# Sums of squares of queries and keys as two products of a rounded high part and a rest

## The reference, cut to what matters

```
h = rmsnorm(x, norm1_g[i])
u = h @ w_in[i]
...
heads = lambda t: t.reshape(b, s, ATTN_HEADS, HEAD_DIM)
qf = rmsnorm(heads(q), q_g).astype(jnp.float32) * (HEAD_DIM ** -0.5)
kf = rmsnorm(heads(k), k_g).astype(jnp.float32)
```

## Time and profile before

| | us |
|---|---|
| median of 3 runs | 1605.55 (1605.2 to 1606.04) |
| the profiled execution, its own time | 1606.08 |
| span of its trace | 1604.2 |
| PE busy in the span | 1580.6 (99%) |
| DVE, ACT, POOL busy | 909.7, 762.8, 645.4 |

### The profile page before, as it was taken

The page is one execution under the profiler, slowest core; times in us unless marked ns, Lnnn a source line. Parts: engine busy times, 40 slices in busy tenths (PEclk is TensorE's granted clock), DMA queues, the critical chain, the costliest instruction groups (busy, mean ns, idle before and its releaser), DMA issues.

```text
span 1604.2 us, 19275 instructions
## 1 busy us (share of the span) xinstructions
PE 1580.6 (99%) x7352; PEld 1262.7 (79%) x7352; DVE 909.7 (57%) x1310; ACT 762.8 (48%) x1204; POOL 645.4 (40%) x323
## 2 busy tenths in 40 slices
PE   7999999999999999999999999999999999999999
PEld 5776778787878888888877777787878788888887
DVE  4578859577755555522227788586678554554000
ACT  5557667476343333332244666765744433333221
POOL 3432221223445555554443312213144555555443
PEclk9999999999999999999999999999999999999999
DMA  5532144453223233233324222454532233232333
GB/s 169 132 100 93 49 124 145 145 150 100 92 92 103 93 98 99 92 95 99 95 92 132 89 76 66 121 157 135 153 98 92 93 94 103 93 102 92 98 96 112
DMA packets 57371, 170.86 MB, mean 107 GB/s; under 512 B 5984, under 2 KB 11872, under 8 KB 57280
## 3 DMA queue, kind: packets, MB, share of 16 engines
q1 hardware_dynamic: 56896, 168.88, 34.0%
q0 software_dynamic: 384, 0.75, 0.4%
HBM read 166.24 MB, written 3.38 MB: 106 GB/s over the span
## 4 chain that ended last, share of the span: by engine, by line
PE 84%; DMA 5%; DVE 3%; issue 3%; POOL 2%; ACT 1%; SPq 1%; DVEq 0%; POOLq 0%; ACTq 0%
PE banks L1170 25%; PE banks L1172 25%; PE banks L1171 25%; DMA sb_w_raw<-w_in 3%; PE banks L1257 2%; PE banks L1248 2%; PE banks L1268 2%; DMA sb_e<-sum_rows 1%; PE banks L1320 1%; PE banks L1228 1%; POOL sb_xc L474 1%; DVE sb_w_lo L847 1%; SPq L339 1%; ACT sb_w_hi L527 0%; DMA sb_x_stream<-x_t 0%
## 5 line engine op out<-in xcount | busy, mean ns | idle before, releaser
L439 POOL TENSOR_TENSOR sb_w_lo<-sb_w_raw,sb_w_hi 128x1024 fp32r<-128x1024 f32 x200 | 482.1, 2411 | 598.9 <-ACT sb_w_hi L527 598.9
L527 ACT ACTIVATE sb_w_hi<-sb_w_raw 128x1024 fp32r<-128x1024 f32 x256 | 271.2, 1059 | 700.1 <-PE banks L1172 648.7
L1170 PE MATMUL banks<-sb_h_hi,sb_w_hi 128*128 128x512 f32 x1344 | 541.7, 403 | 13.1 <-POOL sb_w_lo L439 11.4
L1171 PE MATMUL banks<-sb_h_lo,sb_w_hi 128*128 128x512 f32 x1344 | 524.4, 390 | 0.0
L1172 PE MATMUL banks<-sb_h_hi,sb_w_lo 128*128 128x512 f32 x1344 | 524.4, 390 | 0.0
L1170 PEld LDWEIGHTS banks<-sb_h_hi,sb_w_hi 128*128 128x128 f32 x1344 | 252.7, 188 | 85.2 <-issue 29.7
L1171 PEld LDWEIGHTS banks<-sb_h_lo,sb_w_hi 128*128 128x128 f32 x1344 | 252.9, 188 | 56.5 <-issue 6.5
L1172 PEld LDWEIGHTS banks<-sb_h_hi,sb_w_lo 128*128 128x128 f32 x1344 | 252.7, 188 | 54.2
L1135 DVE TENSOR_TENSOR banks<-banks,sb_rstd 128x512 f32<-128x512 f32 x88 | 61.5, 699 | 133.3 <-PE banks L1172 124.2
L1170 PE MATMUL banks<-sb_ff_hi,sb_w_hi 128*128 128x512 f32 x352 | 136.9, 389 | 0.0
L1171 PE MATMUL banks<-sb_ff_lo,sb_w_hi 128*128 128x512 f32 x352 | 136.9, 389 | 0.0
(11 more groups left out here) (206 smaller groups left out, 2212.9 us busy)
## 6 DMA issues: line engine op xcount, KB each, us to landing
sb_w_raw<-w_in SPq DMA_DIRECT2D x88, 512.0 KB, 3.6
sb_w_raw<-w_up SPq DMA_DIRECT2D x88, 512.0 KB, 3.5
sb_w_raw<-w_out SPq DMA_DIRECT2D x32, 512.0 KB, 3.6
sb_w_raw<-w_down SPq DMA_DIRECT2D x32, 512.0 KB, 3.5
sb_e<-sum_rows SPq DMA_DIRECT2D x16, 512.0 KB, 6.1
sb_bias_t<-bias_rows SPq DMA_DIRECT2D x16, 448.0 KB, 5.8
sb_exp_cs<-sum_rows SPq DMA_DIRECT2D x32, 192.0 KB
sb_w_raw<-w_down SPq DMA_DIRECT2D x16, 384.0 KB, 3.1
```

The costliest lines, as they stand in the source:

```text
L439: g.tensor_tensor(WLO[:, n % 2, :], W[:, n % 2, :], WHI[:, n % 2, :].bitcast(F32), ALU.subtract).then_inc(w_lo.handle, 1)
L527: sc.activation(WHI[:, n % 2, :], W[:, n % 2, :], ACT.Copy).then_inc(w_hi.handle, 1)
L1170: mm(out, whi, hhi, start=start, stop=False)
L1171: mm(out, whi, hlo, start=False, stop=False)
```

## The change

`qk_sum` becomes two fp32r products that accumulate in one bank: `HEADONES`, an fp32r copy of the constant, times a rounded square `QSH`, and times the rest `QSL`. ACT now writes its square, rounded to fp32r, to `QSH`. DVE gets a new step `square_low(n)`, two instructions: the full float32 square `QSF` of the raw tile, and `QSF - QSH`. It stands after the evacuation of tile n (and at n = 0 after the squaring of rstd and `setup()`), ahead of `qk_scale` and `split_low`. The three new buffers have two slots each, so from n = 2 both engines wait for the sum of tile n-2. ACT makes the fp32r copy of the constant once, in layer 0 at n = 0, between rounding chunk 2 and the first square. PE waits for it, for the rounded square and for the rest.

```
+    HEADONES = sb("head_ones", [P, P], F32R)
-    sb("to_lines", [P, 168])
+    sb("to_lines", [P, 40])
...
+                ("qs_high", 64, [P, 2, SEQ], F32R), ("qs_low", 68, [P, 2, SEQ], F32R), ("qs_full", 72, [P, 2, SEQ], F32),
...
-                sc.activation(QKSQ[:, n, :], (Q, K)[n // 4][:, n % 4, :], ACT.Square).then_inc(qk_sq.handle, 1)
+                if layer == 0 and n == 0:
+                    act.wait_ge(con_landed.handle, 16)
+                    sc.activation(HEADONES[:, :], con["headones"], ACT.Copy).then_inc(headones_done.handle, 1)
+                if n >= 2:
+                    act.wait_ge(*qk_ss.at(n - 1))
+                sc.activation(QSH[:, n % 2, :], (Q, K)[n // 4][:, n % 4, :], ACT.Square).then_inc(qk_sq.handle, 1)
...
+        def square_low(n):
+            src = (Q, K)[n // 4][:, n % 4, :]
+            if n >= 2:
+                dve.wait_ge(*qk_ss.at(n - 1))
+            dve.wait_ge(*evac[TILE_BANK["qk", n][0]].at(TILE_BANK["qk", n][1] + 1))
+            v.tensor_tensor(QSF[:, n % 2, :], src, src, ALU.mult).then_inc(qk_sq_full.handle, 1)
+            dve.wait_ge(*qk_sq_full.at(n + 1))
+            dve.wait_ge(*qk_sq.at(n + 1))
+            v.tensor_tensor(QSL[:, n % 2, :], QSF[:, n % 2, :], QSH[:, n % 2, :].bitcast(F32), ALU.subtract)\
+                .then_inc(qk_sq_low.handle, 1)
...
                 if n == 0 and layer == 0:
                     setup()
+                square_low(n)
                 if n >= 2:
                     qk_scale(n - 2)
...
         def qk_sum(n):
             b, k = TILE_BANK["qk", n]
+            pe.wait_ge(headones_done.handle, 1)
             pe.wait_ge(*qk_sq.at(n + 1))
+            pe.wait_ge(*qk_sq_low.at(n + 1))
...
-            mm(bank(6 + n % 2), con["headones"], QKSQ[:, n, :], start=True, stop=True).then_inc(qk_ss.handle, 1)
+            mm(bank(6 + n % 2), HEADONES[:, :], QSH[:, n % 2, :], start=True, stop=False)
+            mm(bank(6 + n % 2), HEADONES[:, :], QSL[:, n % 2, :], start=False, stop=True).then_inc(qk_ss.handle, 1)
```

More of the change, by code:

```diff
@@ L224, in build_trunk @@
     FHI, FLO, FG, FV, FS, FP = (rm[n] for n in ("ff_hi", "ff_lo", "ff_gate", "ff_val", "ff_silu", "ff_prod"))
+    QSH, QSL, QSF = (rm[n] for n in ("qs_high", "qs_low", "qs_full"))
     def mixed(part, k):
@@ L266, in build_trunk @@
     qk_high, qk_low = sem("qk_high", 8), sem("qk_low", 8)
+    headones_done, qk_sq_full, qk_sq_low = sem("headones_done"), sem("qk_sq_full", 8), sem("qk_sq_low", 8)
     r_col = sem("r_col", 1)
```

## The result

The changed kernel takes 1617.14 us (median of 5 runs, 1616.2 to 1617.45), the kernel before 1605.4 (5 runs, 1604.7 to 1606.04): ratio 1.0072, 95% interval 1.006 to 1.0083. It is slower by 11.7 us (0.7%), where 4.7 were forecast; the time lies outside the stated range of 1605.5 to 1613.5 us. The span of the profiled execution is 1615.3 us, 11.1 more than before.

The account below looks back on a forecast made before the run. PE was taken as the bound. Mid-stream savings of 4.5 us against costs of 3.6, 3.9 and 1.7 and nothing at tile 7 gave +4.7 us, forecast 1610.3 us against the median of 1605.55, range 1605.5 to 1613.5.

Parts of the forecast that it names:

- What bounds the kernel: Whole kernel: PE, busy 1580.6 of 1604.2 us; time is won only by taking work from PE, lost when PE waits.
- What PE saves: All 16 sums: two fp32r matmuls of 0.23 replace 0.86 us, saving 6.5 us if every operand is on time.
- The sums in mid-stream: Tiles 1-4 and 6 in layer 0, 1-6 in layer 1: rest stands behind POOL but is covered; -4.5 us.
- The first sum of layer 0: Head of layer 0: full square waits for POOL's second subtraction, rest ends at 31.25; costs +3.6 us.
- The first sum of layer 1: Head of layer 1: full square and rest each go behind a POOL subtraction; costs +3.9 us.
- Rival (b): Head of layer 1: DVE's rest goes ahead of POOL, cost 1.5 instead of 3.9; 1607.9 us; chance 0.17 with smaller variants.
- The sum of tile 5: Layer 0: a late weight chunk delays ACT's square, then POOL and the rest; +1.7 us, bounds 1.5 to 2.0.
- The sum of tile 7: Both layers: only 16 dt matmuls cover it, so the rest comes slightly late and the sum gains nothing.
- Rival (a): DVE is not held up by POOL in these places: -3.0 us, 1602.5 us; chance 0.12.
- the sum itself: Whole kernel: -4.5 + 3.6 + 3.9 + 1.7 + 0 = +4.7 us on the span; forecast's chance 0.52.
- rival (c): PE's clock falls in the new waits of about 4 us: 1.4 us, paid once or twice, 1611.7 or 1613.1; chance 0.13.

Follow-up runs that it names:

- dve_work_only: Kernel before, fp32 product untouched, plus DVE's two new instructions with their waits, PE not waiting for them; 1605.32 us, ratio 0.9999.
- products_only: Changed kernel without DVE's two new instructions; the second product takes the rounded square again; 1600.35 us, ratio 0.9968 to the kernel before.
- bias_later: Changed kernel with the DMA of the bias rows issued one chunk later; 1614.15 us, ratio 1.0056 to the kernel before.
- pool_yields: Changed kernel, POOL holding its subtraction for chunk 3 until DVE has made the layer's first rest; 1611.72 us, ratio 1.0037 to the kernel before.
- fill_pe: Changed kernel with unused fp32r matmuls ahead of PE's three long waits; 1611.5 us, ratio 1.0036 to the kernel before.
- all_three: Changed kernel, ACT making the full square in a PSUM bank, rest ahead of setup, bias-row DMA one chunk later; 1598.74 us, ratio 0.9961 to the kernel before.

## Why the prediction was wrong, point by point

- *What bounds the kernel*: right. Every microsecond lost is one in which PE waits or runs slowly, and DVE's extra work is free where PE does not wait (dve_work_only).
- *What PE saves*: right. 5.94 instead of 6.34 us per tile in mid-stream; 4.9 us in all without the rest (products_only), and of the remaining 1.6 the wait on the late chunk 7 explains 1.0 and one of 0.43 at the head of layer 1 most of the rest; the prediction had seen that chunk only as a cause of the wait at tile 5.
- *The sums in mid-stream*: right. The rest stands still for 2.6 us and ends with POOL, and PE's cover is enough.
- *The first sum of layer 0*: place and cause right, the order wrong. The full square did not stand behind POOL's second subtraction; it ran at 28.16, POOL's subtraction took 0.8 us longer for it, and the rest alone stood still, until 31.58. I had 31.25, and that it came so close is in part luck: one stop fewer for DVE, one for POOL that I had not thought of. PE waited 4.32.
- *The first sum of layer 1*: right as worked out, with each instruction behind a subtraction and a wait of 4.38. Rival (b) is out: DVE did not get its turn.
- *The sum of tile 5*: cause right (bias_later takes that wait away), size too small, 2.6 instead of 1.9 us of waiting. ACT got the chunk at 62.79, 7.2 us later than before (its load took 12.2 instead of 11.6 us), and PE was done with the tile ahead of the sum 5.3 later (its last matmul there starts at 64.12, at 58.86 before): 1.9 us between the two shifts, where I had 1.4.
- *The sum of tile 7*: it waited 0.47 instead of 0.2 in each layer.
- Rival (a) is out: rows of both layers show DVE standing still.
- *The step that failed* is the sum itself, in which a wait cost its length and a cold start and the clock had no term. It was rival (c), at 0.13, and priced too low as well: at most two times 1.4 us, where three waits were followed by 13, 8 and 8 to 9 slow matmuls, 6.0 us. The reason given against it, that these waits are short beside the 10 us of rest at the start, was an argument from the one case that the trace had, and even 2.3 us were enough (pool_yields). The rule of the Trainium skill named there (TensorE: Matmul & The Clock Gate, "HAM oscillation") stood on the side of the rival, and the traces agree with it that an idle PE comes back at the slow clock: 0.50 after every wait of 2.30 us or more in the changed stages of all kernels here. They differ from it in that these waits, the shortest ones, are shorter than the gaps that the section warns of. Behind waits of 1.15 us or less in these stages no matmul was slow.

The forecast with this term is 1610.3 + 6.0 = 1616.3, against 1617.1. The kernel with the same waits and no slow clock takes 1611.5 (fill_pe), 1.2 above the forecast; the waits at tile 5 and the dt tiles, 0.7 and 0.5 longer than worked out, are as large as that.

## What to carry to other kernels

When a change puts a new wait of some microseconds on a busy matrix engine (2.3 were enough here), price it as the wait plus the matmuls that run at 1.2 GHz behind it; here the second part was half of the loss. Before moving work to DVE, look at what POOL does at that time: here an instruction with both inputs in SBUF took up to POOL's whole time on top of its own (2.6 to 2.9 instead of 0.7 us), or held POOL up in turn, and one input in a bank freed it (0.69 us at all 16 places). The same idea, with the full square made by ACT in a bank, is 6.0 us faster than the kernel before (all_three) where the change is 11.7 slower.

## What the runs showed of the hardware

The clock did not take equally long to come back: 13 slow matmuls over 5.7 us after the first wait of layer 0, but 7 over about 3 us in the same place in pool_yields. Why it differs stays open. Behind the tile 5 wait of 2.59 us the first five matmuls still ran at full clock, and the slow clock began only at 68.3 us, 1.2 us after PE had gone back to work. In layer 1 the clock was still at 1.00 until the end of the wait of 4.38 us, and fell only as PE started again (0.50 from 833 us on). So a clock of 1.00 in the window of a wait does not mean that the matmuls behind it are fast. And the DMA of the bias rows (736 KB, 17 us on its way) delays the second load behind it, not the first: before, chunk 6 takes 3.7 us and chunk 7 11.6; in bias_later chunk 7 takes 3.8 and the dt weights 12.3, where they took 5.9 before.
